# Attention head stage: GpSimd scales the probabilities, VectorE shares the copies of the turned ones with ScalarE

## What is computed

```python
s = jnp.einsum('bqkgd,bskd->bkgqs', qblk, k).astype(f32) * (d ** -0.5)
p = softmax_with_sink(s, sink)      # sink only for mixer A
o = jnp.einsum('bkgqs,bskd->bqkgd', p.astype(v.dtype), v)
```

## Time and profile before

| | us |
|---|---|
| median of 3 executions | 789.55 |
| lowest, highest | 788.98, 789.73 |
| time of the profiled execution | 789.94 |
| its span, first to last instruction | 788.0 |

### The profile page before, as it was taken

One profiled execution on the slowest core, in us unless ns is written; L12 is line 12 of the kernel. 1 busy time (PEld: TensorE's weight loads), 2 busy tenths in 40 slices (PEclk: granted clock), 3 DMA queues, 4 the chain that ended last, 5 costly groups with the idle time before them and its releaser, 6 DMA issues.

```text
span 788.0 us, 10974 instructions
## 1 busy us (share of the span) xinstructions
PE 742.7 (94%) x4020; PEld 576.4 (73%) x4020; DVE 582.8 (74%) x968; ACT 502.6 (64%) x834; POOL 50.4 (6%) x36
## 2 busy tenths in 40 slices
PE   4999999899999999999989999989999999999994
PEld 2557777457976888888769888745698788888874
DVE  3258377886656889999868646869676789999965
ACT  3047784484466877777646488557556787777752
POOL 0001342000000000000000035200000000000000
PEclk9999999999999999999999999999999999999998
DMA  9963033978328899999843112386741189999902
GB/s 363 423 237 108 1 133 116 424 274 309 109 107 340 318 377 362 377 376 361 308 181 146 67 54 70 119 362 216 283 153 56 54 319 363 374 364 379 372 17 83
DMA packets 33489, 186.26 MB, mean 236 GB/s; under 512 B 5136, under 2 KB 6288, under 8 KB 16400
## 3 DMA queue, kind: packets, MB, share of 16 engines
q1 hardware_dynamic: 33424, 185.42, 62.4%
HBM read 182.79 MB, written 2.62 MB: 235 GB/s over the span
## 4 chain that ended last, share of the span: by engine, by line
PE 70%; DVE 13%; ACT 10%; issue 5%; DMA 1%; DVEq 0%; ACTq 0%; SPq 0%
PE psum L874 22%; PE psum L903 11%; PE psum L1014 7%; PE psum L1216 5%; PE psum L981 4%; PE psum L926 3%; PE psum L704 3%; PE psum L978 3%; PE psum L852 2%; DVE att L2250 1%; ACT ud L1431 1%; PE psum L755 1%; DVE xbc L2097 1%; ACT split L1407 1%; ACT ring_r L1416 1%
## 5 line engine op out<-in xcount | busy, mean ns | idle before, releaser
L2039 DVE TENSOR_TENSOR split<-ring,split 128x2048 fp32r<-128x2048 f32 x96 | 219.9, 2290 | 26.8 <-ACT split L1532 25.4
L1532 ACT CAST split<-ring 128x2048 fp32r<-128x2048 f32 x96 | 183.5, 1912 | 21.9 <-PE psum L903 14.5
L874 PE MATMUL psum<-split,y_hi 128*128 128x512 f32 x512 | 160.8, 395 | 0.4 <-ACT selT L1505 0.4
L874 PEld LDWEIGHTS psum<-split,y_hi 128*128 128x128 f32 x512 | 93.7, 188 | 18.6 <-issue 0.5
L874 PE MATMUL psum<-split,y_lo 128*128 128x512 f32 x256 | 100.1, 391 | 0.0
L1014 PE MATMUL psum<-ring_r,hT_hi 128*128 128x512 f32 x216 | 74.2, 398 | 1.4 <-ACT row L1641 1.4
L903 PE MATMUL psum<-split,hidT 128*128 128x512 f32 x256 | 69.7, 394 | 1.8 <-DVE hidT_lo L2044 1.8
L903 PEld LDWEIGHTS psum<-split,hidT 128*128 128x128 f32 x256 | 47.3, 188 | 14.2 <-DVE hidT_lo L2044 4.8
L874 PEld LDWEIGHTS psum<-split,y_lo 128*128 128x128 f32 x256 | 48.1, 188 | 10.2
L2480 POOL TENSOR_TENSOR ud<-const,da_hi 128x1024 fp32r<-128x1024 f32 x12 | 27.3, 2294 | 404.2 <-DVE da_lo L2141 397.3
L1014 PEld LDWEIGHTS psum<-ring_r,hT_hi 128*128 128x128 f32 x216 | 40.6, 191 | 10.9 <-issue 2.4
(11 more groups left out here) (308 smaller groups left out, 1431.5 us busy)
## 6 DMA issues: line engine op xcount, KB each, us to landing
ring<-in_w_gu SPq DMA_DIRECT2D x64, 1024.0 KB, 5.2
ring<-in_w_ada SPq DMA_DIRECT2D x40, 1024.0 KB, 6.9
ring<-in_w_down SPq DMA_DIRECT2D x32, 1024.0 KB, 5.3
ring<-in_w_rows SPq DMA_DIRECT2D x12, 1024.0 KB, 4.8
ring<-in_first SPq DMA_DIRECT2D x8, 1024.0 KB, 14.6
ring<-in_w_out SPq DMA_DIRECT2D x8, 1024.0 KB, 5.2
ring<-in_w_xbc SPq DMA_DIRECT2D x8, 800.0 KB, 8.3
par<-in_par SPq DMA_DIRECT2D x1, 1728.0 KB, 13.3
```

What stands on the lines that cost most here:

```text
L874: last = pe.matmul(dst, x[:, g, t, :], w[:, j, :], start=(t == 0 and i == 0), stop=(t == KD - 1 and i == 2))
L1532: act.copy(splits[unit_split(n)][:, 0, :], slot(key)).then_inc(raised("whi", l, p), 1)
L2039: tt(lo, slot(unit_key(l, p, n)), hi.bitcast(F32), ALU.subtract).then_inc(raised("wlo", l, p), 1)
```

## The change

VectorE's `scale` ends with the reciprocal, which raises a new semaphore `rcp`. GpSimd waits for it, multiplies both units of `probs` by the reciprocals, and raises `pn`. Of each pair's two copies of turned probabilities ScalarE keeps the one of unit `2v`; VectorE takes that of `2v + 1`, in its own step `turn`. TensorE's program is not touched.

```diff
                     elif kind == "turn":          # ScalarE
                         v = arg[0]
-                        for u in (2 * v, 2 * v + 1):
+                        for u in (2 * v,):
...
                     elif kind == "scale":         # VectorE
...
-                        dve.reciprocal(att[:, 5, two], den).then_inc(dve_step, 1)
-                        dve.wait_ge(dve_step, dve_steps())
-                        for u in (2 * v, 2 * v + 1):
-                            ins = ts(probs[:, u % 8, 0:w], probs[:, u % 8, 0:w], att[:, 5, u:u + 1], None, ALU.mult)
-                        ins.then_inc(sig["pn"], 1)
+                        dve.reciprocal(att[:, 5, two], den).then_inc(sig["rcp"], 1)
+                    elif kind == "turn":          # VectorE
+                        u = 2 * arg[0] + 1
+                        m, _, kv, i = HEADS[u]
+                        b, chunks = u // 4, 1 if m == 0 else 3
+                        key = ("turn", l, u)
+                        dve.wait_ge(*full(key))
+                        if b >= 2:
+                            dve.wait_ge(*full(("values", l, b - 2)))
+                        dve.tensor_copy(pT[:, b % 2, kv, 0:chunks, i, :],
+                                        bank(key)[:, 0:chunks * P].rearrange("p (c k) -> p c k", k=P)).then_inc(*was_read(key))
...
                 for step in STEPS[l]:              # GpSimd
+                    if step[0] == "scale":
+                        v = step[1]
+                        w = P if HEADS[2 * v][0] == 0 else TOK
+                        pool.wait_ge(sig["rcp"], per["rcp"] * l + v + 1)
+                        for u in (2 * v, 2 * v + 1):
+                            ins = pool.tensor_scalar(probs[:, u % 8, 0:w], probs[:, u % 8, 0:w], att[:, 5, u:u + 1], None, ALU.mult)
+                        ins.then_inc(sig["pn"], 1)
+                        continue
```

More of the change, by code:

```diff
@@ L538, in build @@
                 ("dt_r", 1), ("da", 1), ("bss", 3), ("brs", 3), ("prep", 3), ("ud", 3), ("ud_lo", 3), ("da_lo", 1), ("xd", 3), ("yx", 3),
-                ("mhi", 4), ("mlo", 4), ("mixhi", 4), ("ohi", 1), ("olo", 1), ("wb", 3), ("dtd", 1), ("skip", 3), ("seg", 6), ("in_hi", PARTS + 2), ("in_lo", PARTS + 3), ("zs", 1), ("nb", PAIRS), ("es", PAIRS // 2), ("pn", PAIRS), ("yz", 1), ("yrs", 1), ("yn", 1),
+                ("mhi", 4), ("mlo", 4), ("mixhi", 4), ("ohi", 1), ("olo", 1), ("wb", 3), ("dtd", 1), ("skip", 3), ("seg", 6), ("in_hi", PARTS + 2), ("in_lo", PARTS + 3), ("zs", 1), ("nb", PAIRS), ("es", PAIRS // 2), ("rcp", PAIRS), ("pn", PAIRS), ("yz", 1), ("yrs", 1), ("yn", 1),
                 ("flag", 1), ("top", 2), ("shares", 2), ("chosen", 2), ("hhi", 6),
@@ L2262, in _ @@
                         v = arg[0]
-                        m, t = HEADS[2 * v][0:2]
+                        t = HEADS[2 * v][1]
                         two = slice(2 * v, 2 * v + 2)
-                        w = P if m == 0 else TOK
                         for u in (2 * v, 2 * v + 1):
```

## The result

| | before | after |
|---|---|---|
| median, us | 789.64 | 807.91 |
| lowest to highest | 788.98 to 792.93 | 804.85 to 808.72 |
| executions | 4 | 4 |
| ratio, 95% interval | | 1.0223 (1.0204 to 1.0241) |

What follows compares the result with a forecast made beforehand. The chain was read as TensorE 70%, VectorE 13%, ScalarE 10%, with VectorE leading in parts of the heads. Loop +0.4 and tail +1.8 us a layer, 4.4 over two, took 789.55 to 794.0 us; range 788.5 to 798.5.

Steps and rivals of the forecast that it cites:

- What GpSimd costs: GpSimd's scaling in the heads: 0.65 us wide (bounds 0.37 and 0.83), 0.33 narrow, a wide pair 1.30 us.
- the third rival: Heads loop: at 0.83 us a scaling, `pn` comes 0.36 later in some 5 wide slots a layer; 797.6 us, chance 0.16.
- the 0.4 taken: Heads loop, to the end of ScalarE's rounding (L1407): +0.4 us a layer, between -0.1 and +1.1.
- the 1.8: End of the heads: VectorE's two odd copies behind `out_lo` make TensorE start 1.8 us later in each layer.
- This step does not depend on GpSimd's price: End of the heads: the +1.8 us a layer from copies queued behind `out_lo` was held independent of GpSimd's scaling time.
- The collisions at the gates: Heads: gate products and `gate_scale` each wait up to 0.65 us for GpSimd; its second instruction waits 0.69 for the product.
- GpSimd becomes the loop's bound: Heads loop: GpSimd at 0.83 us a scaling delays `pn` and adds 3.6 us, giving 797.6; chance 0.16.
- Relief wins: Heads: VectorE's 3.3 us a layer come through in full, -3.8 us in all, 785.7; chance 0.11.
- they cancel: Heads: savings on VectorE and ScalarE nearly offset the end's 1.8 us and collisions, giving 790.7; chance 0.18.
- the lower bound: Heads: with GpSimd at 0.37 us a wide scaling, each wide pair's transposes begin 0.0 us later.
- the scores of pair 8: Heads of layer 1: TensorE's scores of this pair ready at 541.5 us without collisions, 542.2 with.
- The first sign: End of the heads: TensorE's wait ahead of the last L1186 grows from 0.90 to over 2 us, released by VectorE's copy.

Runs made afterwards that it cites:

- two-input form: The changed kernel with GpSimd's scaling written as a product of two tensors, the reciprocal broadcast along the row: 795.19 us, ratio 1.0078.
- the constant: The changed kernel with GpSimd multiplying by a constant 0.5 instead of the reciprocal, so probabilities aren't normalised: 808.12 us in one execution.
- copies alone: The kernel before, with VectorE taking the odd copy of each pair and the scaling staying on VectorE: 797.72 us, ratio 1.0111.
- last pairs on VectorE: The changed kernel, but VectorE scales pairs 10 and 11 of each layer itself: 801.24 us, ratio 1.0145.
- scaling alone: The changed kernel, but ScalarE keeps both copies of each pair, so only the scaling moves to GpSimd: 807.96 us, ratio 1.0227.
- the run where nothing waits for GpSimd: The kernel before, with GpSimd also scaling a constant tile into a spare one behind each reciprocal: 796.21 us, ratio 1.0092.

## Why the prediction was wrong

**The step that failed** is the price under "What GpSimd costs": 0.65 us for a wide scaling, with the two-input rows as upper bound, 0.83. Measured are 1.24 alone and 1.39 in the mean, and for a narrow one 0.60 alone and 0.63 in the mean instead of 0.33. The bound rested on the assumption that one input stream can't cost more than two. The two-input form and the constant show the opposite on the same tile: 0.90 against 1.39, and the scalar's place hardly matters. GpSimd's two-input rows of before were sound for their own form: 0.83 is what most two-input scalings took.

**What was right, and what only looks so.** The direction, slower, and the wait of L1171 for GpSimd were as forecast. With the rule of the third rival, the delay of `pn` counted in some five wide slots a layer, a pair of 2.46 us in place of 1.30 adds 5 × 1.16 = 5.8 us to 2.2, so 8.0 a layer and 805.6 in all; the stages grew by 9.2 and 8.4. But that this comes near is luck. The sum has 6.2 us of a layer in the loop and 1.8 in the tail; measured are 3.0 and 3.3 in the loops and 6.1 and 5.0 in the tails. Where a scaling costs 0.90, the time is 795.2, beside the forecast of 794.0; there too the loops are longer than the 0.4 taken, and the tails somewhat shorter than the 1.8.

**"This step does not depend on GpSimd's price"** holds without GpSimd and fails with it; it is the second step that failed. The order alone cost what was worked out, roughly: +1.3 to +1.5 in the five tails where the clock stayed up and TensorE waited for VectorE's copies (copies alone in layer 1, last pairs on VectorE and the two-input form in both), against the +1.8 that I took. What the step left out was that GpSimd scales pairs 10 and 11 in the same stretch. In after, the releaser ahead of the last transposes is GpSimd, and the move of its last pairs to VectorE gives back 4.8 and 3.6 us of the two tails, with the clock in it. With the scaling alone, where no copy stands behind L1928, the tails are as long, so the +1.8 itself isn't in the 18.3 us. In the tail GpSimd also meets L1928, a two-input instruction of 2.29 us: the four scalings took 6.70 us instead of 4.96, so 1.7 longer. In layer 1, two that overlap it took 3.94 instead of 2.46. This is the collision that I priced at the gate products and not here. The Trainium skill's rule on the shared port pair (SBUF — State Buffer, section "Who interferes with whom") covers it; by that rule, the trace agrees at L1928.

**The clock** was not in the sum. It fell to 0.50 within the idle 3.36 us of layer 0 and stood there to 188.2 us. In layer 1 it fell behind idle times of 1.93 and 1.91 us. On the instructions behind the last wait that cost 2.8 and 1.7 us, so some 4.4 of the 18.3. The copies alone show the same at one of two ends.

**The collisions at the gates** came out half as forecast. `gate_scale` grew from 481 to 684 ns. The gate products grew only from 684 to 735, where I had put up to 0.65 us: VectorE doesn't wait for the end of GpSimd's instruction. No `gate_scale` took more than 0.81 us beside GpSimd instructions of 1.24 us and more. The other side was nearer: beside a gate product a wide scaling of GpSimd took 1.67 us instead of 1.24.

**The rivals.** "GpSimd becomes the loop's bound" was the true one in kind, and far too small, 797.6, because it was worked out at 0.83. It also looked for the loss in the loop alone: of the 17.5 us in the four pieces, 11.2 are in the tails (4.4 of them with the clock). "Relief wins" and "they cancel" needed pairs of 0.8 and 1.0 us and had no chance at 2.46. Yet the relief itself was also overrated. In the form that costs 0.90, the loop of layer 0 is 1.2 us longer than before, though VectorE has lost all scalings. The copies that it takes in their place cost that loop 0.8 alone. They were priced at 0.47 us, the pace of two in a row; in the loop they stand alone and take 0.56.

**Small slips of the working.** At the lower bound `pn` comes 0.1 us later and not 0.0, and the scores of pair 8 come out at 541.35 / 542.05 instead of 541.5 / 542.2. Neither moves the forecast by more than 0.2 us a layer.

**What was named as a sign.** L1171 waits for POOL, the gate products are longer than 0.69 us, and the output projection starts late, by 6.1 and 5.0 us instead of 2. The first sign did not come: ahead of the last L1186 there is no wait at all. The wait has moved to L1171, for GpSimd, and only the first of the two copies follows L1928 directly; the second waits for the transposes until 184.12. GpSimd's pairs were not 1.2 to 1.7 us but 2.46 and more; the prediction had named instructions near 1 us as what would put the time well above the range, and that is what came.

**Left open:** whether the lower clock between the stages, and its 2.4 us, belong to the change; why the clock fell behind one wait of 2.06 us and not behind the other; and what puts the loop of layer 1 at the lower clock in six of the runs. No run here shows why GpSimd's form with a scalar is the slower one.

## What to carry to other kernels

A price from an instruction of another form is no upper bound, even if that form has more to read. Where the whole sum hangs on one price that the trace doesn't hold, the range must reach to where that price is twice as high. Here the price was 1.9 times the one taken. And when work moves to another engine, look at the last items of the loop by themselves: no later item hides their latency, and another engine's long instruction may stand just there.

## What the runs showed of the hardware

- GpSimd's `tensor_scalar` on f32 out of and into SBUF took 1.24 us alone for 128x384 and 0.60 for 128x128, so (1.24 - 0.60)/256 = 2.5 ns an element; a constant in place of the scalar's address made it 1.32 in the mean in place of 1.39. `tensor_tensor` with a broadcast second input took 0.83 and 0.40 alone (0.90 and 0.46 in the mean), 1.7 ns an element. The Trainium skill (GPSIMD Engine Reference, section 4.1) has one-input work about at line rate and only two-input work slower; where the page and the measurement differ, the measurement decides, and here the order of the two is the other way round.
- GpSimd beside VectorE: VectorE's scalings out of SBUF grew from 418 to 590 ns and from 481 to 783 in the mean, in the run where nothing waits for GpSimd. Its two-input products hardly grew (684 to 735 at most, in the mean), and GpSimd was the one held up: 2.89 instead of 2.46 us a pair beside a gate product, and by 1.7 us beside the 2.29 us instruction. VectorE's reductions out of PSUM kept their length (551 and 550 ns).
- TensorE's granted clock fell to 0.50 within an idle time of 3.36 us, behind two of 1.9 us, and behind 2.06 us in one of two cases; products at that level took 1.98 us in place of 1.08.
